# One-hot rows of a product-key router: four plain rows in one VectorE instruction, gated rows on three engines, and the next stage's gates loaded from ScalarE's queue

## What is computed

```python
s1 = einsum("bshc,hkc->bshk", q[..., 0, :], keys_1)      # 8 heads, 128 keys for each half
s2 = einsum("bshc,hkc->bshk", q[..., 1, :], keys_2)
v1, i1 = top_k(s1, 16);  v2, i2 = top_k(s2, 16)
top_score, pos = top_k(v1[..., :, None] + v2[..., None, :], 16)      # over the flattened pairs
experts = take_along_axis(i1 * 128 + i2, pos);  gates = softmax(top_score)
y = sum over heads and picks of  gates * gelu(expert_down[experts] . x) * expert_up[experts]
```

## Time and profile before

| | us |
|---|---|
| time before, median of 3 runs | 3178.32 (3176.21 to 3180.08) |
| the profiled execution, whole | 3169.57 |
| the profiled execution, its span | 3167.9 |
| `peer_route` from the first `keep` to the next stage's first matmul | 871.0 to 1167.6 in the span |

### The profile page before, as it was taken

The page is one execution under the profiler, slowest core; times in us unless marked ns, Lnnn a source line. Parts: engine busy times, 40 slices in busy tenths (PEclk is TensorE's granted clock), DMA queues, the critical chain, the costliest instruction groups (busy, mean ns, idle before and its releaser), DMA issues. The chain is left out here.

```text
span 3167.9 us, 42380 instructions
## 1 busy us (share of the span) xinstructions
PE 2985.1 (94%) x14292; PEld 2422.8 (76%) x14292; DVE 2139.6 (68%) x4227; ACT 1282.2 (40%) x1960; POOL 526.8 (17%) x664
## 2 busy tenths in 40 slices
PE   7999999988988889999999999999998899989997
PEld 5678876877777777788888888888877677856886
DVE  5574435346788958888888888888883682545333
ACT  4443343223355642344444444444444332455222
POOL 1023450003477740000000000000001030034000
PEclk8999999999999999999999999999999999989998
DMA  2220002322233354444333334443332212200331
GB/s 105 74 67 28 21 24 94 107 93 98 83 140 140 137 213 135 133 133 132 128 121 124 123 126 132 132 126 124 124 130 80 74 41 67 93 1 12 122 95 72
DMA packets 138195, 317.01 MB, mean 100 GB/s; under 512 B 9296, under 2 KB 74960, under 8 KB 135888
## 3 DMA queue, kind: packets, MB, share of 16 engines
q1 hardware_dynamic: 135440, 281.38, 27.5%
q10 hardware_dynamic: 2624, 33.93, 2.6%
HBM read 275.43 MB, written 39.85 MB: 100 GB/s over the span
## 5 line engine op out<-in xcount | busy, mean ns | idle before, releaser
L197 DVE TENSOR_TENSOR split<-raw,split 128x1024 fp32r<-128x1024 f32 x172 | 209.7, 1226 | 435.0 <-ACT split L188 434.6
L188 ACT ACTIVATE split<-raw 128x1024 fp32r<-128x1024 f32 x220 | 231.5, 1058 | 637.6 <-PE merge L214 193.0
L2172 PE MATMUL up<-up_high,weight_high 128*128 128x512 f32 x700 | 272.3, 389 | 0.0
L2173 PE MATMUL up<-up_low,weight_high 128*128 128x512 f32 x700 | 272.3, 389 | 0.0
L2174 PE MATMUL up<-up_high,weight_low 128*128 128x512 f32 x700 | 272.3, 389 | 0.0
L365 POOL TENSOR_TENSOR xl<-col,xh 128x512 fp32r<-128x512 f32 x8 | 10.0, 1271 | 1073.1 <-ACT xh L337 1073.1
L1867 POOL TENSOR_SCALAR hot<-count,second 128x128 f32<-128x128 f32 x256 | 172.7, 689 | 36.8 <-PE score L1748 25.7
L1748 PEld LDWEIGHTS score<-hot,hot 128*128 128x128 f32 x1024 | 135.1, 200 | 54.9 <-POOL hot L1867 31.2
L1748 PE MATMUL score<-hot,hot 128*128 128x128 f32 x1024 | 142.9, 288 | 34.3 <-POOL hot L1867 19.1
L1918 DVE TENSOR_SCALAR hot<-count,first,gate 128x128 f32<-128x128 f32 x512 | 172.9, 401 | 0.0
L2301 PE MATMUL dt<-xh,split 128*128 128x512 f32 x416 | 162.0, 390 | 1.8 <-ACTq L2419 1.8
(11 more groups left out here) (510 smaller groups left out, 7859.9 us busy)
## 6 DMA issues: line engine op xcount, KB each, us to landing
raw<-in_stream SPq DMA_DIRECT2D x440, 512.0 KB, 3.6
gates<-stage ACTq DMA_DIRECT2D x16, 2048.0 KB, 6.7
gate<-gates SPq DMA_DIRECT2D x32, 1024.0 KB, 8.0
h<-in_x SPq DMA_DIRECT2D x4, 512.0 KB, 6.1
h<-in_x SPq DMA_DIRECT2D x1, 2048.0 KB, 8.5
h_saved<-h SPq DMA_DIRECT2D x1, 2048.0 KB, 7.5
h<-h_saved SPq DMA_DIRECT2D x1, 2048.0 KB, 14.2
rows<-h SPq DMA_DIRECT2D x4, 512.0 KB, 2.6
```

The lines of the kernel that those rows point to most:

```text
L188: act.activation(g.high[t % slots], g.raw[:, t % RAW, :], ACT.Copy).then_inc(g.high_split, 1)
L197: dve.tensor_tensor(g.low[t % slots], g.raw[:, t % RAW, :], g.high[t % slots], ALU.subtract).then_inc(g.low_split, 1)
L2172: pe.matmul(bank, wh, uh, start=start, stop=False, skip_group_check=True)
L2173: pe.matmul(bank, wh, ul, start=False, stop=False, skip_group_check=True)
```

## The change

Plain rows: DVE now makes all four plain rows of a quad in one compare of two broadcast tensors. Gated rows: ACT makes row 3 (distance to `first`, then relu with a per-partition scale of minus the gate and a bias of the gate); DVE makes row 0, and in every fourth quad row 1 too; POOL makes the rest, two rows or one, with compare and multiply. ACT copies the negated gates once a tile to a new buffer `less`. SPREAD goes from (4, 4, 3, 2) to (4, 3, 2, 2), so that 5 `down` tiles run at the end in place of 3. The load of the next stage's first gates moves from the end of SP's queue to ACT's queue, behind the second of these five; SP waits for one stage buffer's stores only, ahead of the load of `h`.

```diff
-SPREAD = (4, 4, 3, 2)
+SPREAD = (4, 3, 2, 2)
+def by_vector(n):
+    return 2 if n % 4 == 3 else 1
...
+    less = g.at("less", R + 56.5, [P, P])
...
# SP
-                for s in range(2):
-                    sp.wait_ge(stored[s], 16 * S // GROUP // 2)
-
-                sp.dma_start(g.gate[:, :, :, :], g.gates[:, :, 0:4, :].rearrange("n p e t -> p n e t"))\
-                  .then_inc(g.first_gates, 16)
+                sp.wait_ge(stored[1], 16 * S // GROUP // 2)
                 sp.dma_start(g.h[:, :, :], saved).then_inc(g.rows_back, 16)
# PE, multiply(n)
-                    pe.wait_ge(third_made, n + 1)
+                    pe.wait_ge(pool_made, n + 1)
+                    pe.wait_ge(last_made, n + 1)
# ACT
+                def negate(t):
+                    act.activation(less[:, :], gate[:, t * P:t * P + P], ACT.Copy, scale=-1.0).then_inc(negated, 1)
...
-                    act.activation(hot2[:, n % 4, QUAD - 1, :], count[:, :], ACT.Abs, scale=-1.0,
-                                   bias=second[:, t:t + 1]).then_inc(apart, 1)
+                    act.activation(hot1[:, n % 4, QUAD - 1, :], count[:, :], ACT.Abs, scale=-1.0,
+                                   bias=first[:, t:t + 1]).then_inc(apart, 1)
...
+                    act.wait_ge(negated, n // PER_TILE + 1)
                     act.wait_ge(apart, n + 1)
-                    hot = hot2[:, n % 4, QUAD - 1, :]
-                    act.activation(hot, hot, ACT.Relu, scale=-1.0, bias=1.0).then_inc(third_made, 1)
+                    t = n * QUAD + QUAD - 1
+                    hot = hot1[:, n % 4, QUAD - 1, :]
+                    act.activation(hot, hot, ACT.Relu, scale=less[:, t % P:t % P + 1],
+                                   bias=gate[:, t:t + 1]).then_inc(last_made, 1)
...
+                        act.wait_ge(last_made, t * PER_TILE)
+                    negate(t)
...
+                    if j == n_spread + 1:
+                        for s in range(2):
+                            act.wait_ge(stored[s], 16 * S // GROUP // 2)
+
+                        act.dma_start(g.gate[:, :, :, :], g.gates[:, :, 0:4, :].rearrange("n p e t -> p n e t"))\
+                           .then_inc(g.first_gates, 16)
# POOL
-                    for k in range(BY_POOL):
+                    for k in range(by_vector(n), QUAD - 1):
                         at = n * QUAD + k
-                        ins = pool.tensor_scalar(hot2[:, n % 4, k, :], count[:, :], second[:, at:at + 1], None,
-                                                 ALU.is_equal)
-                    ins.then_inc(second_made, 1)
+                        ins = pool.tensor_scalar(hot1[:, n % 4, k, :], count[:, :], first[:, at:at + 1],
+                                                 gate[:, at:at + 1], ALU.is_equal, ALU.mult)
+                    ins.then_inc(pool_made, 1)
# DVE
-                    for k in range(QUAD):
+                    at = slice(n * QUAD, n * QUAD + QUAD)
+                    dve.tensor_tensor(hot2[:, n % 4, :, :], count[:, :].unsqueeze(1).to_broadcast([P, QUAD, N_KEYS]),
+                                      second[:, at].unsqueeze(2).to_broadcast([P, QUAD, N_KEYS]),
+                                      ALU.is_equal).then_inc(second_made, 1)
+                    for k in range(by_vector(n)):
                         at = n * QUAD + k
                         ins = dve.tensor_scalar(hot1[:, n % 4, k, :], count[:, :], first[:, at:at + 1],
                                                 gate[:, at:at + 1], ALU.is_equal, ALU.mult)
-                    for k in range(BY_POOL, QUAD - 1):
-                        at = n * QUAD + k
-                        ins = dve.tensor_scalar(hot2[:, n % 4, k, :], count[:, :], second[:, at:at + 1], None,
-                                                ALU.is_equal)
                     ins.then_inc(first_made, 1)
```

More of the change, by code:

```diff
@@ L1658, in peer_route @@
     saved = nc.dram_tensor("h_saved", [S, D], F32, kind="Internal").ap().rearrange("(t p) d -> p t d", p=P)
-    FIRST, BY_POOL = 3, 2
+    FIRST = 3
     per_half, per_pick, steps_of = 5 * TT, 5 * HEADS, 13
@@ L1663, in peer_route @@
     (passed, pool_passed, act_passed, q_read, scored, s_read, key_picked, key_kept, counted, summed, picked, step, grown,
-     chosen_made, turned, kept, activated, second_made, first_made, third_made, apart, product, read, h_saved) = (
+     chosen_made, turned, kept, activated, second_made, first_made, pool_made, last_made, apart, negated, product, read, h_saved) = (
         g.sem(x) for x in (
@@ L1667, in peer_route @@
             "counted", "summed", "picked", "pick_step", "exp_done", "chosen", "turned", "kept", "activated", "second_hot",
-            "first_hot", "second_hot_by_act", "apart", "product", "read", "h_saved"))
+            "first_hot", "first_hot_by_pool", "first_hot_by_act", "apart", "negated",
+            "product", "read", "h_saved"))
     stored = [g.sem(f"stored{s}") for s in range(2)]
```

## The result

The changed kernel takes 3208.11 us (median, 3205.15 to 3210.84) against 3178.27: the ratio is 1.0101, with a 95% interval of 1.0089 to 1.0113. It is 30 us slower, where 14 us faster was forecast, and outside the range (its end was 3201). Its profiled execution took 3207.26 us, with a span of 3205.4. The two profiled executions are 37.7 us apart, the medians 29.8: that of before was 9 us under its median, so the traces overstate the difference a little. The route from the first `keep` to L1367 is steadier: 296.65 us in the kernel before and 296.69 in e4, which changes nothing in it but the gates' load (the most that tiles of the same code were seen to differ by is 1.3 us each, in e12).

The account below looks back on a forecast made before the run. VectorE's list was taken to set the pace of tiles 0 to 2, GpSimd to bound the last. -29.3 + 4.1 + 0.3 + 10.8 = -14.1 us gave 3164.2 us against the median; 8-in-10 range 3141 to 3201.

Parts of the forecast that it names:

- the gates' load: Load of the next stage's first gates, moved to ACT's queue: forecast nought, at most 8 us if its cover were gone.
- VectorE's rows: VectorE's row work in each quad: 0.92 us in place of 1.22, saving 9.6 us of VectorE time a tile.
- The bare tiles: Two more `down` tiles run bare at the end, 5.4 us each: +10.8 us.
- ScalarE's step: ScalarE's second step with two per-partition operands: some 0.2 us more a quad, 6.4 a tile, hidden.
- GpSimd's row: A GpSimd gated row with two scalars and two operations: 0.685 us taken, bounds 0.60 to 0.90.
- The hold: VectorE's tensor_tensor delaying GpSimd's rows: 0 to 0.46 us for each of 32 a tile, 0.2 taken.
- The sum: Tiles 0 to 2 -29.3 us, last tile +4.1 and +0.3, end +10.8: together -14.1 us.
- c: GpSimd's time for a quad: forecast 1.40 us, against 1.27 in the kernel before.
- GpSimd's path in tile 0: GpSimd's time in a tile with five splits, with waits and turn: 65 us, just under VectorE's 67.
- the open price: Unmeasured cost of GpSimd's new two-scalar, two-operation row: between 0.60 and 0.90 us, 0.685 taken.
- The first rival: GpSimd's row list bounds every tile, lasting 128c + 58.5 together; at c = 1.72, +22 us, giving 3200; chance 0.20.
- the break-even: GpSimd's time for a quad from which the change loses, if GpSimd sets every tile: 1.55 us.

Follow-up runs that it names:

- e4: The kernel before with only the first gates' load moved from SP's queue to ScalarE's: ratio 0.9996 to the kernel before.
- e12: Changed kernel with SPREAD (4, 4, 4, 2), GpSimd making one gated row a quad, two in every fourth quad of tiles 0 to 2: 3149.29 us, ratio 0.9920.
- e2: Changed kernel with GpSimd's gated rows comparing only, no gate multiplied in: ratio 0.9952 to the kernel before.
- e5: Changed kernel with GpSimd's gated rows multiplying by an immediate 1.0 in place of the gate: ratio 1.0008 to the kernel before.
- e1: Changed kernel with VectorE's four plain rows made by four tensor_scalars in place of the one compare: ratio 1.0042 to the kernel before.

## Why the prediction was wrong, by its own steps

**VectorE's rows: right.** The compare took 0.69 us in the median, and a quad with one gated row, where nothing held it, 0.86 to 0.95 from one compare to the next (0.60 + 0.26 = 0.86 forecast); busy time in tile 0 was 56.8 us, forecast 57.9. The saving was real, but on an engine that then waited.

**The bare tiles and the gates' load: right.** +10.9 against +10.8, and nought against nought (e4). ScalarE's step cost 0.18 us, hidden (its rows were the last to be ready in no quad).

**GpSimd's row: the first step that failed.** I took VectorE's price for the second scalar and operation, 0.05 us, "since it is the same pair of instructions". It is the same instruction on another engine. GpSimd paid 0.19 (e2, e5), in the middle of my bounds of 0.60 to 0.90, and the value taken should have gone by GpSimd's own rows: a select with no scalar at 0.29, a row with one at 0.59. 0.783 against the 0.685 that I took adds 1.75 x 0.10 = 0.17 us a quad.

**The hold: the second.** I took 0.2 us a quad, on the argument that rows slip into VectorE's gaps. Measured, a row's mean is 1.074 against its 0.783 alone: 0.29 us a row, 0.51 a quad, so 0.31 more than taken. The one GpSimd row that I had beside a long tensor_tensor was held for 0.46, and I reasoned it down. The argument was half true: in the last tile, where VectorE waits much, the hold is 1.75 x (0.950 - 0.783) = 0.29 us a quad. And I laid all of it on the compare. Two thirds of it stayed without one (e1: 0.984 - 0.786 = 0.20 a row).

**The sum.** c was 237.9 / 128 = 1.86 us a quad, not 1.40 (by the rows' mean, 1.75 x 1.074 = 1.88; they overlap a little). I had GpSimd's path in tile 0 at 65 us, 2 under VectorE's 67, so 0.06 us more in c was enough to turn the order round; I let the open price move the last tile alone. With 1.86 the same sum gives 32 x 1.86 + 11.9 + 3 + 5.5 = 80, and measured are 79.5. So VectorE's saving never reached tiles 0 to 2: -29.3 us were forecast there, +10.9 measured. The first rival's rule, 128c + 58.5 for the tiles, gives 296 with it; measured are 290. It put the break-even at 1.55, and e2 bears that out from the other side: its c is 188.6 / 128 = 1.47 and it is faster than before. In e5 c is 208.8 / 128 = 1.63 and the ratio 1.0008, so the real break-even is near 1.6. So the rival's mechanism was right and its threshold nearly, its price of 1.72 was still low, and its chance of 0.20 was far too low for a threshold inside the bounds that I had written down: rows of 0.77 with the hold of the earlier trace rows on a third of the rows already reach it.

**Who was late before: a misreading.** I read the 31.2 us that the view puts down to L1867 as GpSimd being often the last of the three row makers. By the ends of the rows, VectorE was the last in 127 of the 128 quads of the kernel before, ScalarE in one and GpSimd in none: the same trap as in the profile after. It cost the sum nothing, since VectorE's list was taken as the pace; but the full GpSimd of the last tile was seen from its idle time alone.

**What the rule of the skill adds.** The Trainium skill, "SBUF — State Buffer", section "SBUF: two separate sides", names both kinds of VectorE instruction that shut GpSimd out: those with two SBUF inputs and those in a two-port mode. I had used the first half. The runs agree with the first, and rows are held beside tensor_scalars too (0.94 against 0.79 us in e1); whether those ran in such a mode no run here shows. The runs don't show a wait for the whole of each instruction: GpSimd lost 0.51 us a quad, where VectorE's list in it was 0.92 long. Nor does the row, which I called agreement: it had started first, and it was held for 0.46 us under instructions of 0.62 and 0.31.

**The idle columns.** The last tile of the kernel before had said it: GpSimd with 0.5 us of idle time in 64 rows. There, work was put on a full engine, for a saving on another full one. In tiles 0 to 2 GpSimd had 10.5 to 12.7 us idle between its rows, and the change put 16.0 to 17.3 us more on it; the sum stood on VectorE's path there.

## What to carry to other kernels

Before work moves to an engine that has no idle time, price the new instruction by that engine's own rows and count what its neighbour's instructions do to it; where the break-even lies inside the bounds of an unmeasured price, the forecast is open, whatever the middle value says. When three engines make parts of one product, the pace is that of the fullest list, and the same faster instruction can be a loss or a gain by a fraction of a row on another engine (1.0095 and 0.9953 here). The fix was found by reading busy times per tile and moving rows until three engines were within 4 us.

## What the runs showed of the hardware

- A GpSimd tensor_scalar of 128x128 in fp32 takes, at its shortest, 0.60 us with one per-partition scalar and one operation, 0.71 with a second operation by an immediate, and 0.78 with a per-partition scalar for it. VectorE pays 0.05 us for both (274 and 324 ns, the kernel before).
- Beside VectorE's list, its search included, such rows are held: on average by 0.13 us (one scalar, beside tensor_scalars: 0.728 against 0.597), 0.26 (one scalar, beside the compare: 0.860 against 0.597), 0.20 (two scalars, tensor_scalars) and 0.29 (two scalars, the compare). Of the two-scalar rows in the changed kernel the 35 with nothing of VectorE over them took 0.783 to 0.792 us, and so did nine that had only the search's one-input instructions (MAX8, MATCH_REPLACE8, FIND_INDEX8) or `keep`'s copies over them: 0.784 to 0.788.
- A ScalarE activation of 128x128 takes 0.30 us with immediates, 0.40 with one per-partition operand and 0.48 with two.
- A tensor_tensor compare of two broadcast operands costs VectorE what its other tensor_tensors of that size do: 0.69 us for 128x512 (0.68 at L2148 and L2162), 0.41 for 128x256 (medians).
